# Attention items taken two at a time, with the score banks reused for their transpositions

## What is computed

```
x = x + 0.5 * swiglu(rmsnorm(x, g1), w1_in, w1_out)             # width 2816
h = rmsnorm(x, g_mix) @ w_in                                    # q, k, v, gates, merge gates
# NSA: 8 heads in 2 groups, head size 64, for each query tile of 128:
o_c = softmax(q @ kc.T) @ vc          # 31 compressed keys
o_s = softmax(q_r @ ks.T) @ vs        # "selected" blocks: with 512 tokens, all causal ones
o_w = softmax(q_r @ kw.T) @ vw        # window of 512: causal
y_nsa = g0 * o_c + g1 * o_s + g2 * o_w
# dilated: 4 heads, one softmax over the keys of dilations 1, 4 and 16
y_dil = sum over groups of alpha * o
x = x + (gm0 * (y_nsa @ w_nsa) + gm1 * (y_dil @ w_dil)) @ w_out
x = x + 0.5 * swiglu(rmsnorm(x, g2), w2_in, w2_out)
return rmsnorm(x, g_final)
```

## Time and profile before

| | |
|---|---|
| median of 3 runs (lowest, highest) | 1175.52 us (1174.7, 1175.61) |
| the profiled execution | 1176.76 us, its span 1175.0 us |
| TensorE busy | 1163.5 us, 99% of the span |
| VectorE, ScalarE, GpSimd busy | 550.2, 392.2, 158.7 us |
| granted TensorE clock, mean | 0.998 |
| from the first transposition of the attention to the last values | 443.4 to 666.3 us |
| distance between starts of dense matmuls, 512 and 256 wide | 0.23 and 0.12 us |

### The profile page before, as it was taken

How to read it: one execution, slowest core, us unless ns; L and a number is a source line. 1 busy time by engine, 2 the same in 40 slices (tenths; PEclk the granted TensorE clock), 3 DMA queues, 4 the chain that set the end, 5 groups by cost and what they waited for, 6 DMA issues and landing times.

```text
span 1175.0 us, 16417 instructions
## 1 busy us (share of the span) xinstructions
PE 1163.5 (99%) x6675; PEld 953.6 (81%) x6675; DVE 550.2 (47%) x834; ACT 392.2 (33%) x515; POOL 158.7 (14%) x190
## 2 busy tenths in 40 slices
PE   9999999999999999999999999999999999999997
PEld 6888888888888987777778888888888888888886
DVE  6544344463333567656664444653544444432123
ACT  6323323232223233443436422233523232321112
POOL 1000000000111481356661000021000000000000
PEclk9999999999999999999999999999999999999999
DMA  7332333223336831243231233333333333222221
GB/s 229 108 107 78 101 107 89 78 74 99 99 98 144 202 83 40 61 86 65 58 82 29 73 99 90 108 108 90 108 107 91 87 107 103 77 106 77 103 72 73
DMA packets 192228, 111.46 MB, mean 95 GB/s; under 512 B 31984, under 2 KB 186016, under 8 KB 192176
## 3 DMA queue, kind: packets, MB, share of 16 engines
q1 hardware_dynamic: 187616, 104.97, 32.9%
q0 software_dynamic: 4400, 5.61, 1.8%
q10 hardware_dynamic: 160, 0.14, 0.0%
HBM read 105.71 MB, written 2.10 MB: 92 GB/s over the span
## 4 chain that ended last, share of the span: by engine, by line
PE 96%; DVE 2%; DMA 1%; SPq 1%; ACT 0%; issue 0%; ACTq 0%; DVEq 0%
PE ps L1370 22%; PE ps L1372 21%; PE ps L1371 21%; PE ps L1526 3%; PE ps L1525 3%; PE ps L1527 3%; PE ps L1454 3%; PE ps L1453 3%; PE ps L1452 3%; PE ps L1679 2%; PE ps L1602 2%; PE ps L1650 2%; PE ps L1402 1%; PE ps L1404 1%; PE ps L1408 1%; PE ps L1621 1%
## 5 line engine op out<-in xcount | busy, mean ns | idle before, releaser
L967 DVE TENSOR_TENSOR w_lo<-w_raw,w_hi 128x2048 fp32r<-128x2048 f32 (+5 forms) x111 | 225.0, 2027 | 395.4 <-ACT w_hi L714 395.2
L1370 PE MATMUL ps<-xg_hi,w_hi 128*128 128x512 f32 x936 | 367.6, 393 | 0.2 <-DVE square L1122 0.2
L1372 PE MATMUL ps<-xg_hi,w_lo 128*128 128x512 f32 x936 | 364.5, 389 | 0.0
L1371 PE MATMUL ps<-xg_lo,w_hi 128*128 128x512 f32 x936 | 364.4, 389 | 0.0
L714 ACT ACTIVATE w_hi<-w_raw 128x2048 fp32r<-128x2048 f32 (+3 forms) x99 | 179.4, 1812 | 348.2 <-PE ps L1372 201.6
L1370 PEld LDWEIGHTS ps<-xg_hi,w_hi 128*128 128x128 f32 x936 | 175.7, 188 | 38.9 <-issue 3.0
L1372 PEld LDWEIGHTS ps<-xg_hi,w_lo 128*128 128x128 f32 x936 | 175.7, 188 | 36.9
L1371 PEld LDWEIGHTS ps<-xg_lo,w_hi 128*128 128x128 f32 x936 | 175.7, 188 | 35.8
L756 ACT ACTIVATE tmp_a<-tmp_a 128x512 f32<-128x512 f32 x44 | 27.8, 632 | 124.2 <-DVE tmp_a L1029 124.2
L1452 PE MATMUL ps<-w_hi,p_hi 128*128 128x512 f32 x176 | 69.2, 393 | 0.0
L1454 PE MATMUL ps<-w_hi,p_lo 128*128 128x512 f32 x176 | 68.6, 390 | 0.0
(11 more groups left out here) (221 smaller groups left out, 1388.6 us busy)
## 6 DMA issues: line engine op xcount, KB each, us to landing
w_raw<-in_ffn_w_in SPq DMA_DIRECT2D x86, 512.0 KB, 5.0
w_raw<-in_w_in SPq DMA_DIRECT2D x32, 512.0 KB, 5.2
w_raw<-in_ffn_w_out SPq DMA_DIRECT2D x22, 512.0 KB, 4.2
w_raw<-in_ffn_w_out SPq DMA_DIRECT2D x16, 384.0 KB, 3.6
w_raw<-in_w_in SPq DMA_DIRECT2D x24, 256.0 KB, 4.4
w_raw<-in_ffn_w_out SPq DMA_DIRECT2D x16, 320.0 KB, 4.1
w_raw<-in_w_out SPq DMA_DIRECT2D x8, 512.0 KB, 4.0
x_nat<-in_x SPq DMA_DIRECT2D x8, 256.0 KB, 4.6
```

The lines of the kernel that those rows point to most:

```text
L967: lo = V.tensor_tensor(w_lo[:, s, c], w_raw[:, s, c], w_hi[:, s, c].bitcast(F32), ALU.subtract)
L1370: mm(out, ah, bh, start=(first and i == 0), stop=False)
L1371: mm(out, ah, bl, start=False, stop=False)
L1372: last = mm(out, al, bh, start=False, stop=(final and i == len(pairs) - 1))
```

## The change

The items are taken in rounds of two, n and n + 1 with n even (17 rounds, the last with one item). In a round TensorE does both transpositions, then the values of n - 2 and n - 1, then the scores of n + 2 and n + 3, then both dense pieces. Transpositions of an item go to the banks of its own scores (`item_banks`), so the scores of n + 2 wait for ScalarE's copy of item n (`pt_act`) in place of its exponential, and the transpositions no longer wait for the copy before. Banks 4 and 5 come free: dense chunks alternate between banks 7 and 5 and wait for the chunk before the last to be read, and the sums of the values alternate between 6 and 4. The compressed item becomes item 5. Its values are one product for each group in place of two. `FILL` gets a written-out count: two quarters or halves of a chunk for each item up to n = 9, four for each item of the rounds 10, 12, 16, 20 and 22, otherwise one and three. ScalarE and VectorE follow in rounds. The core of the diff:

```diff
-        ITEMS.insert(4, ("cmp", 0))
+        ITEMS.insert(5, ("cmp", 0))
...
+        WHOLE = (10, 12, 16, 20, 22)
...
+            count = 2 if n < 10 else 4 if n - n % 2 in WHOLE else (1, 3)[n % 2]
...
         def bank_of(c):
-            return 7 if c >= N_PRE else 5 if c == N_CH1 else c % 4
+            return (7, 5)[(c - N_PRE) % 2] if c >= N_CH1 else c % 4
+
+        def y_bank(pair):
+            return (6, 4)[pair % 2]
+
+        def item_banks(n):
+
+            b = 2 * (n % 2)
+            return slice(b, b + 2)
...
         def act_attend(act, a, b):
-            for n in range(a, b):
-                act_copy_probs(act, n)
-                if n + 2 < b:
-                    act_exp(act, n + 2)
-                if n > a and ends_pair(n - 1) is not None:
-                    act_y(act, n - 1)
-                c = filled(n - 1)
+            def split_after(n):
+                c = filled(n)
                 if c is not None and ends_unit(c):
                     act_split(act, MIX0 + CH[c][1] + 2)
-                if splits_y(n) is not None:
-                    act_split_y(act, splits_y(n))
+
+            for n in range(a, b, 2):
+                split_after(n - 1)
+                act_copy_probs(act, n)
+                if n + 1 < b:
+                    act_copy_probs(act, n + 1)
+                for nn in (n - 2, n - 1):
+                    if nn >= a and ends_pair(nn) is not None:
+                        act_y(act, nn)
+                for nn in (n + 2, n + 3):
+                    if nn < b:
+                        act_exp(act, nn)
+                split_after(n)
+                for nn in (n, n + 1):
+                    if splits_y(nn) is not None:
+                        act_split_y(act, splits_y(nn))
...
         def dve_attend(dve, a, b):
             dve.wait_ge(gate_ready, 1)
-            dve_factor(dve, a)
-            for n in range(a, b):
-                c = filled(n - 1)
-                if c is not None:
-                    dve_chunk(dve, c)
+            for n in range(a, b, 2):
+                dve_factor(dve, n)
                 if n + 1 < b:
                     dve_factor(dve, n + 1)
-                if n + 2 < b:
-                    dve_prepare(dve, n + 2)
-
-                for unit, half in SPLITS.get(n, ()):
-                    dve_split(dve, MIX0 + unit, half=half)
-                if splits_y(n - 1) is not None:
-                    dve_split_y(dve, splits_y(n - 1))
-            for unit, half in SPLITS.get(b, ()):
-                dve_split(dve, MIX0 + unit, half=half)
+                if filled(n - 1) is not None:
+                    dve_chunk(dve, filled(n - 1))
+                if n in SPLITS:
+                    dve_split(dve, MIX0 + SPLITS[n], half=0)
+                for nn in (n, n + 1):
+                    if splits_y(nn - 2) is not None:
+                        dve_split_y(dve, splits_y(nn - 2))
+                for nn in (n + 2, n + 3):
+                    if nn < b:
+                        dve_prepare(dve, nn)
+                if n in SPLITS:
+                    dve_split(dve, MIX0 + SPLITS[n], half=1)
+                if filled(n) is not None:
+                    dve_chunk(dve, filled(n))
...
-            elif part[0] == 0 and bank_of(c) == 7:
-                pe.wait_ge(proj_read, c)
+            elif part[0] == 0 and c > N_PRE:
+                pe.wait_ge(proj_read, c - 1)
...
             if n >= 2:
-                pe.wait_ge(exp_ready, n - 1)
+                pe.wait_ge(pt_act, n - 1)
...
             pe.wait_ge(scaled_ready, n + 1)
-            if n:
-                pe.wait_ge(pt_act, n)
-            else:
-                pe.wait_ge(proj_read, N_PRE)
...
+            pair = 0 if it[0] == "cmp" else pair_of(n)
+            yb = y_bank(pair)
+            if pair > 1:
+                pe.wait_ge(y_read, pair - 1)
...
         def pe_attend(pe, a, b):
             pe_fill(pe, -1)
-            for n in range(a, b):
+            for n in range(a, b, 2):
                 pe_transpose_probs(pe, n)
-                if n + 2 < b:
-                    pe_scores(pe, n + 2)
-                late = n > a + 1 and ITEMS[n - 1][0] == "cmp"
-                if n > a and not late:
-                    pe_values(pe, n - 1)
-                if n in FILL:
-                    pe_fill(pe, n)
-                if late:
-                    pe_values(pe, n - 1)
+                if n + 1 < b:
+                    pe_transpose_probs(pe, n + 1)
+                for nn in (n - 2, n - 1):
+                    if nn >= a:
+                        pe_values(pe, nn)
+                for nn in (n + 2, n + 3):
+                    if nn < b:
+                        pe_scores(pe, nn)
+                for nn in (n, n + 1):
+                    if nn in FILL:
+                        pe_fill(pe, nn)
```

More of the change, by code:

```diff
@@ L456, in build @@
         N_QKV = sum(c < N_CH3 for c, _, _ in PIECES)
-        QKV_STEPS, LAST_STEP = N_NSA, len(ITEMS) - 1
+        WHOLE = (10, 12, 16, 20, 22)
         FILL, done = {}, 0
[L459 to L464, removed]
+        for n in range(-1, len(ITEMS) - 1):
+            count = 2 if n < 10 else 4 if n - n % 2 in WHOLE else (1, 3)[n % 2]
             took = [piece for piece in PIECES[done:done + count] if piece[0] == PIECES[done][0]]
@@ L480, in build @@
         assert all(max(fill_of(N_CH2 + 2 * hh)) >= LAST_OF[hh] - 2 for hh in range(3))
-        SPLITS = {0: [(CH[C_Q + 3][1] + 2, 0)], 1: [(CH[C_Q + 3][1] + 2, 1)]}
+        SPLITS = {0: CH[C_Q + 3][1] + 2}
         for n in FILL:
             if filled(n) is not None and ends_unit(filled(n)):
[L485 to L488, removed]
+                assert n + 2 - n % 2 not in SPLITS
+                SPLITS[n + 2 - n % 2] = CH[filled(n)][1] + 2
         def by_class(name):
@@ L498, in bank_of, with pair_of @@
         def bank_of(c):
-            return 7 if c >= N_PRE else 5 if c == N_CH1 else c % 4
+            return (7, 5)[(c - N_PRE) % 2] if c >= N_CH1 else c % 4
[4 more added lines that the diff above has]
+            return slice(b, b + 2)
+        def pair_of(n):
+            return ITEMS[n][1] if n < N_NSA else HPG + (n - N_NSA) // CLS
         def wo_bank(m):
@@ L834, in act_copy_probs @@
                 nk = width_of_item(it) if it[0] == "nsa" else T
-                nc.scalar.activation(both[:, :, 0:nk], ps[:, 4:6, 0:nk], ACT.Copy).then_inc(pt_act, 1)
+                nc.scalar.activation(both[:, :, 0:nk], ps[:, item_banks(n), 0:nk], ACT.Copy).then_inc(pt_act, 1)
         def act_y(act, n):
             act.wait_ge(pv_psum, n + 1)
-            src, dst = ps[:, 6, :], y[:, ends_pair(n), :]
+            src, dst = ps[:, y_bank(ends_pair(n)), :], y[:, ends_pair(n), :]
             if n >= N_NSA:
@@ L1636, in pe_transpose_probs @@
                         at = (g * TT + qt) * P
-                        last = nc.tensor.transpose(ps[:, 4 + g, qt * P:qt * P + P], probs[:, e, at:at + P], ident)
+                        last = nc.tensor.transpose(ps[:, b + g, qt * P:qt * P + P], probs[:, e, at:at + P], ident)
                 last.then_inc(trans_psum, 1)
@@ L1644, in pe_transpose_probs @@
                         at = h * T + block_ * P
-                        last = nc.tensor.transpose(ps[:, 4 + h, to * P:to * P + P], probs[:, e, at:at + P], ident)
+                        last = nc.tensor.transpose(ps[:, b + h, to * P:to * P + P], probs[:, e, at:at + P], ident)
                 last.then_inc(trans_psum, 1)
@@ L1649, in pe_transpose_probs @@
                 for kt in range(width_of_item(it) // P):
-                    last = nc.tensor.transpose(ps[:, 4 + i, kt * P:kt * P + P],
+                    last = nc.tensor.transpose(ps[:, b + i, kt * P:kt * P + P],
                                                probs[:, e, i * T + kt * P:i * T + kt * P + P], ident)
@@ L1655, in pe_cmp_values @@
             rows = slice(hh * NC, hh * NC + NC)
-            for at, w in ((0, T),) if opens else ((0, 3 * P), (3 * P, P)):
-                for g in range(2):
-                    last = mm(ps[g * DH:g * DH + DH, 6, at:at + w], v_cmp[rows, g, :],
-                              cmp_probs_t[rows, g * T + at:g * T + at + w], start=opens, stop=False)
+            for g in range(2):
+                last = mm(ps[g * DH:g * DH + DH, y_bank(hh), :], v_cmp[rows, g, :], cmp_probs_t[rows, g * T:g * T + T],
+                          start=opens, stop=False)
             return last
@@ L1678, in pe_values @@
                         for g in range(2):
-                            last = mm(ps[g * DH:g * DH + DH, 6, qt * P:qt * P + P], v_nsa[:, kt, i, g * DH:g * DH + DH],
+                            last = mm(ps[g * DH:g * DH + DH, yb, qt * P:qt * P + P], v_nsa[:, kt, i, g * DH:g * DH + DH],
                                       probs_t[:, e, g * T + at + kt * P:g * T + at + kt * P + P],
@@ L1694, in pe_values @@
                 for h in range(2):
-                    last = mm(ps[h * DH:h * DH + DH, 6, c * P + at:c * P + at + w],
```

(1 more changed line is left out.)

7 lines of the change are left out of this document (2 added, 5 removed).

## The result

The changed kernel takes **1178.99 us** (median of 20 executions, 1177.62 to 1181.67) against 1175.26 us before (20 executions beside it): ratio 1.0033, 95% interval 1.0026 to 1.0039. It is slower by 0.33%, 3.7 us. The forecast was 1176.3 us, with a range from 1171.5 to 1181.5 us: the time lies inside the range, but above the stretch of 1174 to 1178.5 us that the forecast itself named.

What follows compares the result with a forecast made beforehand. TensorE, busy 1163.5 of 1175.0 us, was taken to bound the kernel. 1176.76 - 6.8 + 5.2 + 1.0 + 1.4 = 1177.6, adjusted by 1.24 to the median: 1176.3 us, range 1171.5 to 1181.5.

Steps and rivals of the forecast that it cites:

- the seams: On TensorE in the attention, merging items into rounds removes changes between kinds of products: 6.8 us off, bank-7 wait included.
- the copies: Scores of n+2 and n+3 wait for ScalarE's copies of transposed probabilities: 5.2 us added, bounds 0 and 9.
- F: Dense pieces on TensorE, whole array: 16 seams saved at 0.10 us, 1.6 us.
- T: Transpositions on TensorE, whole array: 16 seams saved at 0.09 us, 1.5 us.
- S: Scores on TensorE, 64 rows by 32 columns: 15 merged, one saving nothing, 1.65 us saved.
- The rival of hidden copies: Scores' waits for ScalarE's copies are covered, so the 5.2 us goes: 1171.1 us, chance 0.17.
- the compressed item: Item 5's transposition stalls 1.4 us for VectorE's factors with the clock falling as before; 2.1 without the fall.
- the first round: Second transposition waits 0.6 to 0.7 us for scaled probabilities, a score's copy adds 0.3: 1.0 us, up to 2.
- Covered: Later transpositions find VectorE's factors ready, no stall; tightest in rounds of 256-wide chunks, slack 0.2 to 0.6 us.
- the rival of slow VectorE operations: VectorE late at T(n+3) in the 256-wide rounds, one slow operation in each of five: +5 us, 1181.3, chance 0.18.
- The clock: Rival: TensorE's clock falls in every second round at 1.5 us each: +12 us, 1188, chance 0.11.
- The rule of the Trainium skill on transpositions: Transpositions on TensorE don't count as busy for the clock, which speaks against the new order; no size given.

Runs made afterwards that it cites:

- the pair: Second profiles of the changed kernel and the kernel before, both unedited and without a clock fall in the attention: 1178.02 and 1173.93 us.
- The buffer: Changed kernel with a third buffer for the transposed probabilities, so ScalarE's copy waits for the values of n - 3, not n - 2: 1174.34 us.
- less rotation: GpSimd's rotation of the attention's chunks cut from 512 to 64 columns: 1178.68 us on the changed kernel, 1171.40 on that with third buffer, late splits and late reads.
- the late half splits: Changed kernel with the second half of each VectorE weight split moved behind the next round's factors: 1179.31 us, ratio 1.0026.
- the version with the dense pieces apart: Changed kernel with third buffer and later half splits, order put back to scores(n+2), dense(n), scores(n+3), dense(n+1): 1188.64 us, ratio 1.0107.

## Why the prediction was off

The time lies inside the stated range, yet the sum said +0.8 us and the pair shows +4.1, all misses but the seams' being waits sized too small or left out. That the range held is in part luck: its upper bound was set for VectorE being late in the 256-wide rounds, and there it was not.

**Right: the seams.** 6.15 us against 6.8, a little less saved in sum. F was worth more than I took, T and S less. The Trainium skill (TensorEngine Tiling (Array Packing), Tiling Modes, Key Properties) names the drain without a price; the runs give it one here.

**Right: the copies.** 5.25 us against 5.2, and the waits stand where the round-by-round list put them: 0.39 in round 2, 0.60 in 4, 0.25 in 6, 0.23 to 0.24 in 8, 14 and 20, 0.33 to 0.39 in the others. The buffer took 4.65 us off. The rival of hidden copies is out.

**Mis-sized: the compressed item.** 1.4 us rested on a dense piece at half clock. "Without the clock fall 2.1" stood beside it, and 2.15 is what the fall-free profile has; the first profile, with its fall, has 1.3. The mechanism was right and the condition under which I priced it was one execution's.

**Mis-sized, or not: the first round.** 1.65 us in the pair against 1.0, but 0.7 between the two first profiles. The changed kernel loses 2.1 and 2.2 us to waits in this round in its two profiles; it is the kernel before that differs, with 1.4 us ahead of its first transposition in the profile on which I built, and 0.5 in the other. Both first factors run beside GpSimd's rotation, and it depends on the execution which of them is stretched, as VectorE shows in the second profile of the changed kernel and then in the first, against 3.05 and 1.01 in the earlier trace rows:

```profile
439.86 2.08 DVE L1230 TENSOR_SCALAR probs<-probs,stat 128x128 f32<-128x128 f32 x4
442.06 1.16 DVE L1223 TENSOR_TENSOR stat<-stat,gates 128x4 f32<-128x4 f32 x1
443.26 1.01 DVE L1230 TENSOR_SCALAR probs<-probs,stat 128x128 f32<-128x128 f32 x4
```

```profile
440.20 1.01 DVE L1230 TENSOR_SCALAR probs<-probs,stat 128x128 f32<-128x128 f32 x4
441.33 1.05 DVE L1223 TENSOR_TENSOR stat<-stat,gates 128x4 f32<-128x4 f32 x1
442.41 2.02 DVE L1230 TENSOR_SCALAR probs<-probs,stat 128x128 f32<-128x128 f32 x4
```

**The step that failed: "Covered".** It let the late rounds keep their distance with "two factors of up to 1.4" each and saw the tightest place in the 256-wide rounds. In those nothing waits but the first and the compressed item. The waits, 1.2 us, stand in rounds 16 and 20, the 512-wide ones in which GpSimd rotates. I had the mechanism in hand, as the rival of slow VectorE operations, and dismissed it because "no rope falls in those rounds", without putting the same price into the rounds where it does. The rows of the second profile of the changed kernel ahead of the wait at 576.70, VectorE and then GpSimd:

```profile
573.51 1.05 DVE L1223 TENSOR_TENSOR stat<-stat,gates 128x4 f32<-128x4 f32 x1
574.60 2.04 DVE L1230 TENSOR_SCALAR probs<-probs,stat 128x128 f32<-128x128 f32 x4
```

```profile
572.49 2.05 POOL L662 TENSOR_TENSOR tmp_a<-tmp_a,sin_t 128x512 f32<-128x512 f32 x1 [1.41 <-DMA tmp_a<-pool]
574.69 1.35 POOL L669 TENSOR_TENSOR pool<-tmp_a,tmp_b 128x512 f32<-128x512 f32 x1
```

VectorE loses 1.9 us to the earlier trace rows's prices of 0.17 and 1.01, and GpSimd 0.75 to its usual 1.30, while VectorE's weight split runs (1.22 us from 572.18). By the Trainium skill (SBUF — State Buffer, Who interferes with whom) VectorE and GpSimd share a pair of SBUF ports as an exclusive lock: a scaling in a two-port mode, or a product of two SBUF operands beside a GpSimd instruction that reads SBUF, waits for the other or holds it up, in full. The rows and the two runs with less rotation agree.

**The clock.** Its rival named more falls. Falls do come more often or longer in some executions (of the changed kernel's 20, 8 had a mean clock of 0.996 or less and a median of 1180.7 us; 11 had 0.998 or more and 1178.2), but the difference between the kernels is 4.1 us in the pair with no fall in either, and 3.0 us between the medians at a mean clock of 0.998 or more. So the falls are not the main cause of the loss; about 0.7 of the 3.7 us between the medians goes with them. In this small part the rival was right. What makes one execution fall and another not stays open. The rule of the Trainium skill on transpositions, cited in the prediction, stays untested.

Of the 3.3 us by which the pair differs from the sum, 1.2 are the late rounds, 0.75 the compressed item, 0.65 the first round, 0.65 the seams and 0.05 the copies.

## What to carry to other kernels

When items are merged into rounds, the buffers' depth must grow with them: two halves that were enough for one item at a time cost 5 us here, and a third turned a loss of 0.3% into a gain of 0.2%. A TensorE at 99% with no waits has slack in its neighbours only; price VectorE's work in each round at its slow value wherever GpSimd works beside it, not only where it was seen. And before terms of a few us are weighed against a profile, take a second one: two executions of one kernel differed here by 2.8 us, in a fall of the clock and a first wait. Medians need the same care: sorted by mean clock, a change that seemed worth nothing (the late half splits) or 0.3 us (less rotation) was worth about 1.5.

## What the hardware showed unexpectedly

- TensorE's granted clock fell to 0.5 (1.2 GHz) in the attention for 3.4 us once in the first profile of the kernel before and not in its second; for 6.8 us in the first of the changed kernel and not in its second. A fall of 3.4 us costs about 1.5 us in dense products (an estimate from steps of 0.21 in place of 0.12 us).
- The falls stand in two kinds of place. Of the ten in the attention of all 14 profiles, six begin within 1 us of the end of the compressed item's scores, with no wait directly before them. The other four come within 1.1 us after transpositions had waited for factors: 2.2 us each in the version with the dense pieces apart (falls from 474.2 and 576.6 us), 1.5 and then 0.45 us in the first round of two others. Seven profiles have no fall there; all seven have the scores and six of them waits of 1.3 to 2.2 us, so neither is enough for one.
- VectorE and GpSimd stretch each other by whole instructions: four scalings of 128x128 took 1.01, 2.02 to 2.10 or 3.05 us, a product of four columns 0.17 undisturbed and up to 1.24, and a rotation step 1.30 or 2.05.
- A group of 32-column scores and a dense piece more in the same round cost TensorE 0.40 us, with the step from dense products straight to scores among it.
